# A chunked recurrence in which each chunk starts fourteen steps behind the one before it

## The chip, the cores and the metric

The kernel runs on one core of a Trainium2 chip. The metric is device time of one launch in microseconds. The core has four compute engines, each with its own queue of instructions that it works through in order: TensorE (PE), VectorE (DVE), ScalarE (ACT) and GpSimd (POOL); SyncE (SP) issues most DMAs. Engines wait for one another through semaphores that the program raises and waits for.

## The reference

The model is a block of mixed attention, recurrence, short convolution and an expert lookup, followed by two transformer layers; everything is float32. The change touches only the recurrence of the first block, which runs over 256 context tokens and then 512 latent tokens, in 4 heads of 64 and in both directions:

```python
def step(S, inp):
    r_t, kk_t, v_t, w_t, b_t, k_t = inp
    sa = jnp.einsum('bhij,bhj->bhi', S, kk_t)
    S = S * w_t[:, :, None, :] - sa[..., None] * b_t[:, :, None, :] + v_t[..., None] * k_t[:, :, None, :]
    return S, jnp.einsum('bhij,bhj->bhi', S, r_t)
for d, reverse in enumerate((False, True)):
    ctx_state, y_c = wkv_scan(state0, *c_common, *c_dirs[d], reverse=reverse)
    _, y_l = wkv_scan(ctx_state, *l_common, *l_dirs[d], reverse=reverse)
```

Only the latent tokens' outputs are used; of the context only the state is.

## The kernel before

The recurrence is computed in 12 chunks of 64 tokens, 4 of the context (c = 0 to 3) and 8 latent ones (c = 4 to 11). Both directions and all heads are worked on together, as four 128x128 blocks. A chunk has a part that does not need the state and one that does.

The part without the state (`chunk_pe`, `chunk_act`, `chunk_dve`, `chunk_pool`) goes so:

- Inputs. DVE subtracts the decay sums (L1477), ACT takes exponentials E2, E3, E1 (L1437, L1439, L1441), DVE scales the keys and the queries (L1480, L1484, L1489), POOL scales other keys and copies the values (L1549, L1554), and ACT copies the result into the blocks (L1444).
- PE forms three sets of products, N, M1 and M2 (L1384), four 128x128 matmuls each (for a context chunk M1 and M2 are 64 wide). DVE masks them (L1499, L1502 for N; L1509 and, in latent chunks, L1513 for M1 and M2).
- PE transposes four sets of blocks (L1392: Bt, T0, Kt, Vt) and ACT copies them out of PSUM (L1452).
- The inverse of a triangular matrix follows in four levels l = 1 to 4: products X (L1399), copied by ACT; products A (L1399), added by DVE (L1522); transposes T (L1392), copied by DVE in odd levels (L1526) and by ACT in even ones (L1452). POOL masks the operand of each level (L1541). Last come the products Y and "inverse" (L1399; DVE L1530).

The part with the state (`state_pe`, `state_dve`) has three products with an eviction after each: RH (L1587, L1588; DVE L1627), U (L1595; DVE L1631) and the sum (L1602, L1603; DVE L1635), and then DVE scales the sum into the new state (L1642). A latent chunk also has outputs (L1615 to L1617; DVE L1654). On the profile each float32 matmul counts as two passes, a transpose as one.

Every engine's program for a chunk is a Python generator that yields at the same points, called steps. `chunks` runs two generators by turns, so chunk c and chunk c + 1 are at the same step, and each set of four matmuls of one is followed by the same set of the other. When both have ended, the state parts of c and c + 1 are written one after the other, with the outputs of c between RH and U of c + 1. There are two sets of buffers, and chunk c uses set c % 2, so its inputs wait for the last PE work of chunk c - 2 (`state_filled, (c - 2, "last")`). Each set has its own three PSUM banks; banks 6 and 7 serve the state. A barrier stands before and after the stage.

Of the kernel before, what the change touches and what calls it, by code (L numbers as in the profile page):

```python
# [1369 lines left out]
def chunk_pe(k, p, c):  # L1370
    S, rw = k.S, k.rw
    B, nk = rw.sets[c % 2], 2 if c >= 4 else 1
    yield
    p.wait_ge(S.chunk_kept, (c, "inputs"))
    p.wait_ge(S.chunk_prepared, (c, "inputs"))
    p.wait_ge(S.chunk_copied, (c, "inputs"))
    for step, (name, left, right, w) in enumerate((
            ("N", B.AB, lambda s: B.BB[:, s, :], P),
            ("M1", B.BB, lambda s: B.KR[:, s, 0:nk, :], 64 * nk),
            ("M2", B.KB, lambda s: B.KR[:, s, 0:nk, :], 64 * nk))):  # L1380
        bank = chunk_bank(k, B, c, step)
# [24 lines left out]
    yield
    turned(5, "Kt", B.KB, S.chunk_copied)
    yield
    p.wait_ge(S.chunk_prepared, (c, "values"))
    turned(6, "Vt", B.VB, S.chunk_copied)  # L1410
    yield
    for l in range(1, 5):
        p.wait_ge(S.chunk_prepared, (c, "NTo", l))
        products(4 + 3 * l, f"X{l}", B.NTo, B.Ta, S.chunk_copied)
        yield
        p.wait_ge(S.chunk_copied, (c, f"X{l}"))
        p.wait_ge(S.chunk_copied if l % 2 else S.chunk_kept, (c, f"T{l - 1}"))
        products(5 + 3 * l, f"A{l}", B.Tb, B.Xs, S.chunk_kept)
        yield
        p.wait_ge(S.chunk_kept, (c, f"A{l}"))  # L1420
        turned(6 + 3 * l, f"T{l}", B.Ta, S.chunk_kept if l % 2 else S.chunk_copied)
        yield
    p.wait_ge(S.chunk_copied, (c, "T4"))
    products(19, "Y", B.No, B.Tb, S.chunk_copied)
    yield
    p.wait_ge(S.chunk_copied, (c, "Y"))
    products(20, "inverse", B.Ta, B.Xs, S.chunk_kept)
    yield


def chunk_act(k, p, c):
    S, rw = k.S, k.rw
    B = rw.sets[c % 2]
    if c >= 2:
        p.wait_ge(S.state_filled, (c - 2, "last"))
        p.wait_ge(S.state_ready, c - 2)
    p.e.activation(B.E2, windows(rw.Ls, c), ACT.Exp, scale=-1.0).then_inc(*p.up(S.decay_exp, (c, 2)))  # L1437
    p.wait_ge(S.decay_diff, c)
    p.e.activation(B.E3, B.E3, ACT.Exp).then_inc(*p.up(S.decay_exp, (c, 3)))  # L1439
    if c >= 4:  # L1440
        p.e.activation(B.E1, windows(rw.Ls, c), ACT.Exp).then_inc(*p.up(S.decay_exp, (c, 1)))  # L1441
    p.wait_ge(S.chunk_kept, (c, "keys"))
    for a, h in enumerate(HEAD):
        p.e.activation(B.AB[h, :, h], B.KR[h, :, 0, :], ACT.Copy).then_inc(  # L1444
            *(p.up(S.chunk_copied, (c, "inputs")) if a else p.up(S.scalar_step)))
    if c < 4:
        p.e.activation(B.E1, windows(rw.Ls, c), ACT.Exp).then_inc(*p.up(S.decay_exp, (c, 1)))
    yield

    def copied(step, name, dst):  # L1450
        p.wait_ge(S.chunk_filled, (c, name))
        p.e.activation(flat(dst), chunk_bank(k, B, c, step), ACT.Copy).then_inc(*p.up(S.chunk_copied, (c, name)))  # L1452

    for _ in range(3):
        yield
    for step, name, dst in ((3, "Bt", B.Bt), (4, "T0", B.Tb), (5, "Kt", B.Kt), (6, "Vt", B.Vt)):
        copied(step, name, dst)
        yield
    for l in range(1, 5):
        copied(4 + 3 * l, f"X{l}", B.Xs)  # L1460
        yield
        yield
        if l % 2 == 0:
            copied(6 + 3 * l, f"T{l}", B.Tb)
        yield
    copied(19, "Y", B.Xs)
    yield
    yield


def chunk_dve(k, p, c):
# [14 lines left out]
    if latent:  # L1486
        p.wait_ge(S.decay_exp, (c, 1))
        for d in range(2):
            p.e.tensor_tensor(B.KR[:, SL[d], 1, :], window(rw.Z[:, 0:2, :], c, d), B.E1[:, d], ALU.mult).then_inc(  # L1489
                *(p.up(S.chunk_kept, (c, "inputs")) if d else p.up(S.vector_step)))  # L1490
    else:
        p.in_order()
        p.e.drain().then_inc(*p.up(S.chunk_kept, (c, "inputs")))
    yield
    bank = chunk_bank(k, B, c, 0)
    p.wait_ge(S.chunk_filled, (c, "N"))
# [37 lines left out]
def chunk_pool(k, p, c):  # L1534
# [20 lines left out]
                *(p.up(S.chunk_prepared, (c, "values")) if d and h.start else p.up(S.pool_scaled)))  # L1555
    yield
    yield
    p.wait_ge(S.chunk_kept, (c, "M1", "left") if latent else (c, "M1"))
    off_diagonal(1)
    for _ in range(6):  # L1560
# [13 lines left out]
    return 6 + rw.turn % 2  # L1574


def state_pe(k, p, c, between):

    S, rw = k.S, k.rw
    B, S0 = rw.sets[c % 2], rw.ST[c % 2]  # L1580
    b = state_bank(rw)
    p.claim(("bank", b), S.state_kept, (c, "RH"))
    p.wait_ge(S.state_ready, c - 1)
    p.wait_ge(S.chunk_kept, (c, "inverse"))
    for s in range(4):
        o = k.bank[b][:, s * P:s * P + P]
        p.e.matmul(o, B.M2[:, s, :], B.Vt[:, s, :], start=True, stop=False, skip_group_check=True)  # L1587
        ins = p.e.matmul(o, B.AB[:, s, :], S0[:, s, :], start=False, stop=True, skip_group_check=True)  # L1588
    ins.then_inc(*p.up(S.state_filled, (c, "RH")))
    run(between)  # L1590
    b = state_bank(rw)
    p.wait_ge(S.state_kept, (c, "RH"))
    p.claim(("bank", b), S.state_kept, (c, "U"))
    for s in range(4):
        ins = p.e.matmul(k.bank[b][:, s * P:s * P + P], B.Tb[:, s, :], rw.RH[:, s, :], start=True, stop=True, skip_group_check=True)  # L1595
    ins.then_inc(*p.up(S.state_filled, (c, "U")))
    b = state_bank(rw)
    p.wait_ge(S.state_kept, (c, "U"))
    p.claim(("bank", b), S.state_kept, (c, "sum"))
    for s in range(4):  # L1600
        o = k.bank[b][:, s * P:s * P + P]
        p.e.matmul(o, B.Kt[:, s, :], B.Vt[:, s, :], start=True, stop=False, skip_group_check=True)  # L1602
        ins = p.e.matmul(o, B.Bt[:, s, :], rw.U[:, s, :], start=False, stop=True, skip_group_check=True)  # L1603
    ins.then_inc(*p.up(S.state_filled, (c, "sum" if c >= 4 else "last")))


def outputs_pe(k, p, c):
# [11 lines left out]
    yield  # L1619


def state_dve(k, p, c, between):
    S, rw = k.S, k.rw
    B, S0, S1 = rw.sets[c % 2], rw.ST[c % 2], rw.ST[(c + 1) % 2]
    b = state_bank(rw)
    p.wait_ge(S.state_filled, (c, "RH"))
    p.e.tensor_scalar(flat(rw.RH), k.bank[b], -1.0, None, ALU.mult).then_inc(*p.up(S.state_kept, (c, "RH")))  # L1627
    run(between)
    b = state_bank(rw)
    p.wait_ge(S.state_filled, (c, "U"))  # L1630
    p.e.tensor_copy(flat(rw.U), k.bank[b]).then_inc(*p.up(S.state_kept, (c, "U")))  # L1631
    b = state_bank(rw)
    p.in_order()
    p.wait_ge(S.state_filled, (c, "sum" if c >= 4 else "last"))
# [2 lines left out]
    for s in range(4):  # L1637
        d, g = s // 2, s % 2
        e1 = B.E1[:, d, g, 63:64] if d == 0 else B.E1[:, d, g, 0:1]
        if s == 0:  # L1640
            p.in_order()
        p.e.tensor_scalar(S1[:, s, :], rw.sum[:, s, :], e1, None, ALU.mult).then_inc(  # L1642
            *(p.up(S.state_ready, c) if s == 3 else p.up(S.vector_step)))


def outputs_dve(k, p, c):
# [9 lines left out]
    yield  # L1656


def chunks(k, p, part, state, outputs):

    k.rw.turn = 0
    for c in range(0, 12, 2):
        both = [part(k, p, c), part(k, p, c + 1)]
        while both:
            both = [x for x in both if next(x, x) is not x]
        if state is None:
            continue
# [1926 lines left out]
```

## Time and profile before

| | us |
|---|---|
| median of 3 runs | 4511.9 |
| lowest, highest | 4507.26, 4541.98 |
| profiled execution | 4547.44 |
| its span | 4545.6 |
| mean granted clock of it | 0.855 |

The span is the time from the first to the last instruction in the profiled execution. The twelve chunks lie between 657 us (the first N) and 1028 us of it, after the projections and before the output projection and the expert lookup. A granted clock of 1.00 is 2.4 GHz on TensorE and 0.50 is 1.2 GHz; a value between is a mean over a stretch.

### The profile page before, as it was taken

Reading aid. Unit: us, or ns where it says so; the run is one execution under the profiler, and the core shown is the slowest. Engines: PE = TensorE matmul, PEld = TensorE weight load, DVE = VectorE, ACT = ScalarE, POOL = GpSimd, SP = SyncE. Lnnn points to the kernel's source line nnn. Section 1 sums busy time; section 2 is a strip of 40 time slices with the busy share of each in tenths; the row PEclk is TensorE's granted clock in tenths of the full one; section 3 lists DMA queues with packets and bytes.
Section 4 is the critical chain, followed back from the end, with each engine's and each line's share of the span. In section 5 each row is a group of like instructions: output and inputs, shape, how many; then the busy total and the mean of one; then the engine's idle time right before and its main releaser. Section 6 shows DMA issues by size and latency. Waiting matters only on the chain. (4 is left out here: it accounts for less than half of the span.)

```text
span 4545.6 us, 38958 instructions
## 1 busy us (share of the span) xinstructions
PE 3563.3 (78%) x14192; PEld 2537.7 (56%) x14192; DVE 2238.7 (49%) x4378; ACT 696.2 (15%) x1541; POOL 1408.6 (31%) x1202
## 2 busy tenths in 40 slices
PE   7879957887366667566667898877977889989899
PEld 3446537783122233232545676666765468877687
DVE  2442054443777756755766767777652420032201
ACT  2111022221111111111121101211011210011100
POOL 0640012220266545547534655555520000000000
PEclk9886968998688878888867899978998889997999
DMA  6310300001488878879846899878962024421243
GB/s 193 105 56 5 97 12 1 1 1 48 155 311 311 301 259 298 305 275 370 301 155 240 328 392 360 312 259 299 393 250 65 28 74 148 150 82 38 93 156 104
DMA packets 439283, 833.18 MB, mean 183 GB/s; under 512 B 46451, under 2 KB 281518, under 8 KB 439086
## 3 DMA queue, kind: packets, MB, share of 16 engines
q0 software_dynamic: 147456, 536.94, 32.4%
q1 hardware_dynamic: 291638, 293.76, 20.3%
q8 instruction: 114, 1.87, 0.2%
q14 instruction: 75, 0.61, 0.0%
HBM read 828.44 MB, written 2.17 MB: 183 GB/s over the span
## 5 line engine op out<-in xcount | busy, mean ns | idle before, releaser
L2364 PE MATMUL banks<-arena 128*128 128x256 f32 (+1 forms) x4992 | 1161.0, 392 | 93.6 <-DVE arena L2434 43.4
L2364 PEld LDWEIGHTS banks<-arena 128*128 128x128 f32 (+1 forms) x4992 | 976.8, 197 | 271.9 <-issue 67.3
L1953 POOL DMA_INDIRECT arena<-in_peer_v,arena x512 | 637.4, 1245 | 785.9 <-DVE arena L2062 468.2
L2073 DVE CUSTOM_DVE_ANT_0 arena<-arena 128x1024 f32<-128x1024 f32 x512 | 628.1, 1227 | 236.5 <-DMA arena<-in_peer_u,arena 221.0
L2020 PE MATMUL banks<-arena 128*128 128x512 f32 x768 | 449.7, 729 | 298.0 <-ACT arena L2038 181.7
L1953 POOL DMA_INDIRECT arena<-in_peer_u,arena x512 | 554.9, 1084 | 378.4 <-DVE arena L1905 187.7
L2020 PEld LDWEIGHTS banks<-arena 128*128 128x128 f32 x768 | 166.3, 230 | 552.8 <-issue 330.9
L2062 DVE SCALAR_TENSOR_TENSOR arena<-arena 128x1024 f32<-128x1024 f32 x316 | 406.2, 1285 | 34.9 <-DMA arena<-in_peer_v,arena 25.0
L614 PE MATMUL banks<-arena 128*128 128x512 f32 (+1 forms) x768 | 312.7, 566 | 1.8 <-DVEq L280 1.8
L3130 PE MATMUL banks<-arena 128*128 128x256 f32 x1408 | 310.4, 378 | 0.0
L3172 DVE TENSOR_TENSOR arena<-banks,arena 128x512 f32<-128x512 f32 x44 | 30.5, 692 | 528.1 <-PE banks L2364 527.7
L3130 PEld LDWEIGHTS banks<-arena 128*128 128x128 f32 x1408 | 265.6, 189 | 38.3
L614 PEld LDWEIGHTS banks<-arena 128*128 128x128 f32 x768 | 149.7, 196 | 163.3 <-issue 158.1
L958 PE MATMUL banks<-arena 128*128 128x512 f32 (+1 forms) x320 | 131.1, 557 | 25.4 <-ACT arena L1085 9.8
L2626 PE MATMUL banks<-arena 64*128 64x256 f32 (+6 forms) x384 | 142.6, 482 | 4.4 <-issue 3.2
L2633 PE MATMUL banks<-arena 128*128 128x128 f32 x360 | 87.6, 344 | 65.4 <-ACT arena L2684 34.4
L2640 PE MATMUL banks<-arena 128*128 128x64 f32 (+1 forms) x720 | 134.8, 330 | 2.2 <-DVE arena L2735 2.2
L2640 PEld LDWEIGHTS banks<-arena 128*128 128x128 f32 x720 | 131.0, 259 | 6.0 <-issue 4.8
L3151 ACT ACTIVATE arena<-banks 128x512 f32<-128x512 f32 x44 | 26.3, 597 | 700.0 <-PE banks L2364 699.9
L2669 ACT ACTIVATE arena<-arena 128x256 f32<-128x256 f32 (+3 forms) x128 | 69.4, 542 | 393.3 <-DVE arena L2708 299.2
L2633 PEld LDWEIGHTS banks<-arena 128*128 128x128 f32 x360 | 52.1, 171 | 120.5 <-issue 62.4
L513 POOL TENSOR_TENSOR arena<-arena 128x2048 f32<-128x2048 f32 x16 | 57.3, 3602 | 196.5 <-ACTq L280 104.9
(327 smaller groups left out, 3900.5 us busy)
## 6 DMA issues: line engine op xcount, KB each, us to landing
arena<-in_l_w_gate SPq DMA_DIRECT2D x44, 1024.0 KB, 7.4
arena<-in_l_w_up SPq DMA_DIRECT2D x44, 1024.0 KB, 9.0
arena<-in_l_w_down SPq DMA_DIRECT2D x44, 1024.0 KB, 6.5
arena<-in_ada_w SPq DMA_DIRECT2D x24, 1024.0 KB, 8.5
arena<-in_l_w_qkv SPq DMA_DIRECT2D x24, 1024.0 KB, 6.3
arena<-in_w_in SPq DMA_DIRECT2D x36, 512.0 KB, 4.0
arena<-in_l_w_out SPq DMA_DIRECT2D x16, 1024.0 KB, 5.2
arena<-in_peer_q_w SPq DMA_DIRECT2D x16, 512.0 KB, 4.8
```

The costliest lines, as they stand in the source:

```text
L614: ins = p.e.matmul(k.bank[b][0:m, 0:n], k.W[slot][:, c, 0:m], rhs(c), start=c == 0, stop=c == c_n - 1, skip_group_check=True)
L958: ins = p.e.matmul(k.bank[b][0:m, 0:n], k.W[slot][:, c, 0:m], rhs(c), start=c == 0, stop=c == c_n - 1, skip_group_check=True)
L1953: p.e.indirect_dma_start(e.ring[slot], None, tables[table], bass.IndirectOffsetOnAxis(ap=e.IDX[h][:, t, j:j + 1], axis=0)).then_inc(*p.up( ...
L2020: ins = p.e.matmul(k.bank[b], e.diag[x % 4], e.ring[slot][:, half * T:half * T + T], start=h == 0 and j == 0, stop=h == HEADS - 1 and j == ...
L2062: p.e.scalar_tensor_tensor(out=e.ACC[t], in0=e.ring[slot], scalar=factor, in1=e.ACC[t], op0=ALU.mult, op1=ALU.add).then_inc(*p.up(S.rows_a ...
L2073: p.e.tensor_tensor_reduce(out=e.prod, in0=e.ring[slot], in1=e.H2[:, t, :], scale=1.0, scalar=0.0, op0=ALU.mult, op1=ALU.add, accum_out=e. ...
L2364: ins = p.e.matmul(out, left(c), right(c), start=c == 0, stop=c == c_n - 1, skip_group_check=True)
L2626: ins = p.e.matmul(k.bank[b][:, c0:c0 + keys.shape[1]], x.q, keys, start=True, stop=True, skip_group_check=True)
L2633: ins = p.e.transpose(k.bank[4][:, j * P:j * P + P], a.S[u % 2][:, j * P:j * P + P], k.ident)
L2640: ins = p.e.matmul(k.bank[5][:, 0:x.w], a.PT[u % 2][:, j * P:j * P + P], values, start=j == 0, stop=j == len(x.values) - 1, skip_group_che ...
L2669: p.e.activation(s[:, 0:x.nb], s[:, 0:x.nb], ACT.Exp, bias=low, scale=-1.0, accum_out=cols[:, 2:3]).then_inc(*(p.up(S.weights_exp, key) if ...
L3130: ins = p.e.matmul(k.bank[4 + o // 2][:, o % 2 * TH:o % 2 * TH + TH], w[:, r, P * o:P * o + P], a.hid[:, (i - 1) % 2, TH * r:TH * r + TH], ...
```

## The change

A chunk's generator now goes on through its state part and its outputs: `state_pe` and `state_dve` yield after each of their products, where the outputs of another chunk used to be passed in. `chunks` keeps a list of active chunks. Chunk c joins it at step 14c, and at each step the older one is written before the newer. One step is added near the start of each engine's program of a chunk: PE forms N in a chunk's third step now, two steps after DVE's first work on the inputs, and on ACT the copies into the blocks are a step of their own.

```diff
--- before.py
+++ after.py
@@ -1371,6 +1371,7 @@
     S, rw = k.S, k.rw
     B, nk = rw.sets[c % 2], 2 if c >= 4 else 1
     yield
+    yield
     p.wait_ge(S.chunk_kept, (c, "inputs"))
     p.wait_ge(S.chunk_prepared, (c, "inputs"))
     p.wait_ge(S.chunk_copied, (c, "inputs"))
@@ -1439,6 +1440,7 @@
     p.e.activation(B.E3, B.E3, ACT.Exp).then_inc(*p.up(S.decay_exp, (c, 3)))
     if c >= 4:
         p.e.activation(B.E1, windows(rw.Ls, c), ACT.Exp).then_inc(*p.up(S.decay_exp, (c, 1)))
+    yield
     p.wait_ge(S.chunk_kept, (c, "keys"))
     for a, h in enumerate(HEAD):
         p.e.activation(B.AB[h, :, h], B.KR[h, :, 0, :], ACT.Copy).then_inc(
...
@@ -1587,13 +1591,14 @@
         p.e.matmul(o, B.M2[:, s, :], B.Vt[:, s, :], start=True, stop=False, skip_group_check=True)
         ins = p.e.matmul(o, B.AB[:, s, :], S0[:, s, :], start=False, stop=True, skip_group_check=True)
     ins.then_inc(*p.up(S.state_filled, (c, "RH")))
-    run(between)
+    yield
     b = state_bank(rw)
     p.wait_ge(S.state_kept, (c, "RH"))
     p.claim(("bank", b), S.state_kept, (c, "U"))
     for s in range(4):
         ins = p.e.matmul(k.bank[b][:, s * P:s * P + P], B.Tb[:, s, :], rw.RH[:, s, :], start=True, stop=True, skip_group_check=True)
     ins.then_inc(*p.up(S.state_filled, (c, "U")))
+    yield
     b = state_bank(rw)
...
+LAG = 14
+
+
+def pauses_of(n):
+    for _ in range(n):
+        yield
+
+
+def chunk_steps(k, p, c, part, state, outputs):
+
+    yield from part(k, p, c)
+    if state is None:
+        yield from pauses_of(4 if c >= 4 else 3)
+        return
+    yield from state(k, p, c)
+    if c >= 4:
+        yield from outputs(k, p, c)
+
+
 def chunks(k, p, part, state, outputs):
 
     k.rw.turn = 0
-    for c in range(0, 12, 2):
-        both = [part(k, p, c), part(k, p, c + 1)]
-        while both:
-            both = [x for x in both if next(x, x) is not x]
-        if state is None:
-            continue
-        state(k, p, c, None)
-        state(k, p, c + 1, outputs(k, p, c) if c >= 4 else None)
-        if c >= 4:
-            run(outputs(k, p, c + 1))
+    active, step, c = [], 0, 0
+    while active or c < 12:
+        if c < 12 and step >= c * LAG:
+            active.append(chunk_steps(k, p, c, part, state, outputs))
+            c += 1
+        active = [x for x in active if next(x, x) is not x]
+        assert len(active) < 3
+        step += 1
```

The first place is PE's queue where a latent pair begins. A row is a line, an operation and how many of it follow one another; L1384 (now L1385) is N, M1 and M2, L1392 (now L1393) transposes, L1399 (now L1400) the products of the levels. Before:

```order
L1384 MATMUL banks<-arena 128x128 x24
L1392 MATMUL banks<-arena 128x128 x32
L1399 MATMUL banks<-arena 128x128 x16
L1392 MATMUL banks<-arena 128x128 x8
L1399 MATMUL banks<-arena 128x128 x16
L1392 MATMUL banks<-arena 128x128 x8
```

and with the change, from X2 and A2 of the older chunk on:

```order
L1400 MATMUL banks<-arena 128x128 x8
L1393 MATMUL banks<-arena 128x128 x4
L1400 MATMUL banks<-arena 128x128 x8
L1385 MATMUL banks<-arena 128x128 x4
L1393 MATMUL banks<-arena 128x128 x4
L1385 MATMUL banks<-arena 128x128 x4
L1400 MATMUL banks<-arena 128x128 x4
L1385 MATMUL banks<-arena 128x128 x4
L1400 MATMUL banks<-arena 128x128 x4
L1393 MATMUL banks<-arena 128x128 x12
L1400 MATMUL banks<-arena 128x128 x4
L1393 MATMUL banks<-arena 128x128 x4
```

N, M1 and M2 stood together for both chunks, then all first transposes, then level after level. Now T2, X3 and A3 of the older chunk stand ahead of N of the newer, and M1 and M2 are divided by T3 and X4.

The second place is DVE's queue at the same point. L1477 to L1489 (now L1479 to L1491) prepare inputs, L1499 and L1502 (L1502 and L1505) evict N, L1509 and L1513 (L1512 and L1516) evict M1 and M2, L1522 (L1525) adds A, L1529 copies T of an odd level. Before:

```order
L1477 TENSOR_TENSOR arena<-arena 128x256
L1480 TENSOR_TENSOR arena<-arena 64x4x64 x2
L1484 TENSOR_TENSOR arena<-arena 128x2x64 x2
L1489 TENSOR_TENSOR arena<-arena 128x2x64 x2
L1477 TENSOR_TENSOR arena<-arena 128x256
L1480 TENSOR_TENSOR arena<-arena 64x4x64 x2
L1484 TENSOR_TENSOR arena<-arena 128x2x64 x2
L1489 TENSOR_TENSOR arena<-arena 128x2x64 x2
L1499 TENSOR_TENSOR arena<-banks,arena 128x512 x2
L1502 TENSOR_TENSOR arena<-arena 128x512
L1499 TENSOR_TENSOR arena<-banks,arena 128x512 x2
L1502 TENSOR_TENSOR arena<-arena 128x512
```

and with the change, from the addition of the older chunk's A2 on:

```order
L1525 TENSOR_TENSOR arena<-banks,arena 128x512
L1479 TENSOR_TENSOR arena<-arena 128x256
L1482 TENSOR_TENSOR arena<-arena 64x4x64 x2
L1486 TENSOR_TENSOR arena<-arena 128x2x64 x2
L1491 TENSOR_TENSOR arena<-arena 128x2x64 x2
L1525 TENSOR_TENSOR arena<-banks,arena 128x512
L1502 TENSOR_TENSOR arena<-banks,arena 128x512 x2
L1505 TENSOR_TENSOR arena<-arena 128x512
L1529 COPY arena<-banks 128x512
L1512 TENSOR_TENSOR arena<-banks,arena 64x4x64 x2
L1516 TENSOR_TENSOR arena<-banks,arena 128x256
L1512 TENSOR_TENSOR arena<-banks,arena 64x4x64 x2
```

The additions of A2 and A3 of the older chunk stand around the inputs of the newer, and its copy of T3 stands between the evictions of N and M1.

## Rows read from the trace of the kernel before

**Rows 1.** The page, part 1: busy us, share of the span, number of instructions.
```profile
PE 3563.3 (78%) x14192; PEld 2537.7 (56%) x14192; DVE 2238.7 (49%) x4378; ACT 696.2 (15%) x1541; POOL 1408.6 (31%) x1202
```

**Rows 2.** Windows by round: stretch, its length, busy time of each engine, granted clock, DMA.
```profile
657.00:719.00 62.00, 50.05 (x352) 47.23 (x352) 26.88 (x52) 16.45 (x32) 14.67 (x21) 0.86 0.00 1
719.00:783.00 64.00, 52.48 (x352) 49.44 (x352) 26.40 (x52) 16.41 (x32) 14.33 (x20) 0.82 0.00 1
783.00:847.20 64.20, 53.08 (x400) 50.41 (x401) 31.25 (x68) 17.06 (x35) 14.47 (x20) 0.88 0.00 1
847.20:908.60 61.40, 51.14 (x401) 48.34 (x401) 30.28 (x64) 16.43 (x33) 14.48 (x20) 0.92 0.00 1
...
970.00:1027.80 57.80, 51.05 (x400) 48.23 (x400) 27.20 (x54) 14.21 (x27) 11.88 (x14) 0.93 0.00 1
```

**Rows 3.** Timeline of PE, fourth round: start, length, line, passes, idle time before.
```profile
847.22 2.05 PE L1384 MATMUL banks<-arena 128*128 128x128 f32 x8 [3.45 <-ACT arena L1444]
850.80 6.73 PE L1384 MATMUL banks<-arena 128*128 128x128 f32 x40 [1.53 <-ACT arena L1444]
857.37 2.35 PE L1392 MATMUL banks<-arena 128*128 128x128 f32 x20
...
861.27 3.80 PE L1399 MATMUL banks<-arena 128*128 128x128 f32 x32
864.96 0.66 PE L1392 MATMUL banks<-arena 128*128 128x128 f32 x4
865.85 0.66 PE L1392 MATMUL banks<-arena 128*128 128x128 f32 x4 [0.24 <-DVE arena L1522]
866.35 3.80 PE L1399 MATMUL banks<-arena 128*128 128x128 f32 x32
...
888.20 1.16 PE L1595 MATMUL banks<-arena 128*128 128x128 f32 x8 [0.78 <-DVE arena L1627]
```

**Rows 4.** Timeline of DVE, same stretch.
```profile
847.54 1.29 DVE L1480 TENSOR_TENSOR arena<-arena 64x256 f32<-64x256 f32 x2 [0.50 <-ACT arena L1437]
848.86 0.91 DVE L1484 TENSOR_TENSOR arena<-arena 128x128 f32<-128x128 f32 x2
849.69 0.57 DVE L1489 TENSOR_TENSOR arena<-arena 128x128 f32<-128x128 f32 x2
850.19 1.27 DVE L1499 TENSOR_TENSOR arena<-banks,arena 128x512 f32<-128x512 f32 x2
851.50 0.69 DVE L1502 TENSOR_TENSOR arena<-arena 128x512 f32<-128x512 f32 x1
...
856.05 0.86 DVE L1509 TENSOR_TENSOR arena<-banks,arena 64x256 f32<-64x256 f32 x2
856.95 0.42 DVE L1513 TENSOR_TENSOR arena<-banks,arena 128x256 f32<-128x256 f32 x1
...
865.11 0.69 DVE L1522 TENSOR_TENSOR arena<-banks,arena 128x512 f32<-128x512 f32 x1 [0.20 <-PE banks L1399]
```

**Rows 5.** Timeline of ACT, same stretch.
```profile
847.10 0.42 ACT L1437 ACTIVATE arena<-arena 128x256 f32<-128x256 f32 x1
...
849.80 0.85 ACT L1444 ACTIVATE arena<-arena 64x256 f32<-64x256 f32 x2 [1.68 <-DVE arena L1484]
...
863.26 0.60 ACT L1452 ACTIVATE arena<-banks 128x512 f32<-128x512 f32 x1 [0.30 <-PE banks L1399]
```

**Rows 6.** Windows around a round start and two state phases: the granted clock.
```profile
847.00:857.00 10.00, 8.25 (x45) 8.01 (x46) 8.55 (x19) 1.93 (x6) 4.24 (x8) 0.60 0.00 0
857.00:865.00 8.00, 7.80 (x70) 7.49 (x69) 3.42 (x8) 5.33 (x10) 3.27 (x3) 1.00 0.01 2
...
885.00:894.00 9.00, 5.67 (x45) 4.95 (x43) 3.89 (x9) 0.00 (x0) 0.00 (x0) 1.00 0.00 0
...
764.00:770.00 6.00, 4.70 (x24) 4.22 (x24) 1.04 (x3) 0.00 (x0) 0.00 (x0) 0.72 0.00 0
```

**Rows 7.** POOL's level masks in the stage, from the groups by line.
```profile
L1541 POOL TENSOR_TENSOR arena<-arena 128x512 f32<-128x512 f32 x48 | 52.4, 1091 | 98.3 <-PE banks L1399 66.0 <-DVE arena L1509 29.2
```

More of the change, by code:

```diff
@@ L1574, in state_bank, with state_pe @@
     return 6 + rw.turn % 2
-def state_pe(k, p, c, between):
+def state_pe(k, p, c):
     S, rw = k.S, k.rw
@@ L1596, in state_pe @@
     ins.then_inc(*p.up(S.state_filled, (c, "U")))
+    yield
     b = state_bank(rw)
@@ L1604, in state_pe @@
     ins.then_inc(*p.up(S.state_filled, (c, "sum" if c >= 4 else "last")))
+    yield
 def outputs_pe(k, p, c):
@@ L1619, in outputs_pe, with state_dve @@
     yield
-def state_dve(k, p, c, between):
+def state_dve(k, p, c):
     S, rw = k.S, k.rw
@@ L1627, in state_dve @@
     p.e.tensor_scalar(flat(rw.RH), k.bank[b], -1.0, None, ALU.mult).then_inc(*p.up(S.state_kept, (c, "RH")))
-    run(between)
+    yield
     b = state_bank(rw)
@@ L1631, in state_dve @@
     p.e.tensor_copy(flat(rw.U), k.bank[b]).then_inc(*p.up(S.state_kept, (c, "U")))
+    yield
     b = state_bank(rw)
@@ L1643, in state_dve @@
             *(p.up(S.state_ready, c) if s == 3 else p.up(S.vector_step)))
+    yield
 def outputs_dve(k, p, c):
@@ L1656, in outputs_dve @@
     yield
+LAG = 14
+def pauses_of(n):
+    for _ in range(n):
+        yield
+def chunk_steps(k, p, c, part, state, outputs):
[6 more added lines that the diff above has]
+        yield from outputs(k, p, c)
 def chunks(k, p, part, state, outputs):
     k.rw.turn = 0
-    for c in range(0, 12, 2):
-        both = [part(k, p, c), part(k, p, c + 1)]
-        while both:
-            both = [x for x in both if next(x, x) is not x]
-        if state is None:
-            continue
-        state(k, p, c, None)
-        state(k, p, c + 1, outputs(k, p, c) if c >= 4 else None)
-        if c >= 4:
-            run(outputs(k, p, c + 1))
+    active, step, c = [], 0, 0
[6 more added lines that the diff above has]
+        step += 1
 def rwkv_output_pe(k, p):
```

## The prediction

> **What bounds the kernel now.** The page's first part says how much there is to win: TensorE is busy for 78% of the span, more than any other engine [rows 1]. A window for each of the six rounds of the recurrence then gives its size, 62.0 + 64.0 + 64.2 + 61.4 + 61.4 + 57.8 = 370.8 us, 8% of the span [rows 2] (the fifth round repeats the fourth). A full round holds 51.1 us of PE work in 61.4 us [rows 2]; DVE has 30, POOL 14, ACT 16. So no other engine bounds it, and what could go is the 10.3 us of PE idleness and the part of the 51.1 that runs at half clock. The timeline of PE shows where both lie. A round begins with 3.45 us without work, then N of chunk A, 8 passes in 2.05 us, 1.53 us without work, and 40 passes in 6.73 us [rows 3]; later 32 passes go in 3.69 us (861.27 to 864.96). The granted clock agrees: 0.60 from 847 to 857, 1.00 from 857 to 865 [rows 6]. Half speed thus costs 8.8 us less 48 x 0.112 = 5.4, or 3.4 us per latent round. The rest of the idleness is 0.24 us per level and the state's hand-offs, as the 0.78 us before U [rows 3]. At full clock the work of a latent chunk is (51.1 - 3.4)/2 = 23.9 us.
>
> **The change, part by part.** No instruction of arithmetic is added or removed; no DMA is issued in the stage. Only the order on the four engines changes. Two things are gained: the state's steps and the outputs of one chunk stand between steps of the next, and the inputs of a chunk are prepared while another has work. Three are lost: X and A of a chunk no longer have the partner's same step between them and their eviction at every place, each chunk prepares its inputs by itself (eleven handovers and not five), and the first and the last chunk run alone for 14 steps each.
>
> Durations for the walk:
> - eight passes 0.9 us (a quarter of the 32 passes in 3.69, [rows 3]); a group of four transposes 0.5 (865.85 to 866.35); state products twice 0.9, outputs 2.65 (24 passes at 0.11)
> - A to its transposes: the products end at 864.85 (four groups from 861.27), the addition begins at 865.11 and takes 0.69, the transposes start at 865.85: 1.0 [rows 3, 4]. X or a transpose to ACT and back: 0.2 + 0.6 + 0.06 [rows 5]
> - inputs: from the first exponential at 847.10 to PE's start at 850.80, 3.7 us, with 1.29, 0.91 and 0.57 on DVE between [rows 3 to 5]
> - DVE for N: 850.19 to 852.2, 2.0; each mask pair with its row part 1.25 [rows 4]; POOL 1.1 for a level's mask [rows 7]
>
> Steady state, two latent chunks, time 0 at the end of A2 of the older one c. In that step c-1 has just ended, and c+1 has nothing on PE for its first two steps. So T2 waits for its addition with no cover: 1.0 to 1.5; X3 to 2.4. ACT copies T2 at 1.7 and only then computes the exponentials of c+1, from 2.3; the copy of X3 stands behind them and ends at 4.0. A3 runs 4.06 to 4.95. N of c+1 comes at 2.33 + 3.7 = 6.03. Idle so far: 1.0 + 1.7 + 1.1. N, T3, M1, X4 and M2 then follow without a hole to 10.2, A4 and Bt to 11.7. DVE is behind: queued after the keys' products (5.5) it does A3's addition (6.2), N's three (from 7.2 to 9.2), the copy of T3 (9.9), and the masks of M1 (11.15) and M2 (12.4), and only then A4's addition (13.1). T4 starts at 13.15: idle 1.45. T0 follows, Y waits 0.4 for T4's copy (14.5 to 15.4), Kt, inverse 16.26 to 17.15, Vt, RH 18.15 (0.4 idle) to 20.0, X1 to 20.9, U to 21.9, A1 to 22.8, sum to 24.8, T1, outputs 25.4 to 28.1, X2 to 29.0, and A2 after X2's copy, 29.85 to 30.75. **The period is 30.75 us per chunk, where a round gave 61.4/2 = 30.7** [rows 2]. The state is hidden as meant (RH's eviction lies under X1, U's under A1, the sum's under T1 and the outputs), but waits of about 7 us per chunk stand where 10.3/2 = 5.2 us stood; the half clock's 1.7 us per chunk pays for the difference.
>
> With no outputs the period is 2.65 shorter, and with a context chunk as the newer one DVE's masks are 4 x 0.4 us shorter, of which 1.4 lie on the way to A4's addition. So three periods of 26.7 (chunks 0 to 2 older), one of 28.1 (3 older, 4 newer), seven of 30.75: 80.1 + 28.1 + 215.3 = 323.5 us.
>
> The ends. Chunk 0 alone, at half clock, since PE had stood still before: N 2.05, masks to about +6.3 and the transposes to +8.3, then X1 1.75, 0.86, A1 1.75, 1.0, T1 0.8, X2 1.75, 0.86, A2 1.75: 18.8 us. Chunk 11 alone after its A2: two levels at 0.9 + 0.86 + 0.9 + 1.0 + 0.5 less what overlaps to T4's end (9.8), copy 0.86, Y 0.9, copy 0.86, inverse 0.9, addition 1.0, RH 1.85, 1.0, U 0.9, 1.05, sum 1.85, outputs 2.65: 23.6 us. Sum 18.8 + 323.5 + 23.6 = 365.9 us.
>
> The clock. It fell in every round after PE had waited 3.45 us, and it also fell in a state phase, with no wait there longer than U's 0.78 us [rows 3]: 0.72 on average over the 6 us from 764 to 770, so 3.4 us at half [rows 6]. In the handover above PE waits 3.8 us in three pieces over 6 us, with no piece above 1.7; from 885 to 894, busy 5.67 of 9 us, the fourth round kept the clock [rows 6]. The two speak against one another, so I take the fall at half of the eleven handovers, for the 3.4 us of the shorter case, 1.7 us lost each: 9 us. Bounds: 0 and, if each is as long as at a round's start (847.22 to 857.37, 10.2 us, [rows 3]), 11 x 5.1 = 56. For the lone ends I add 2 (0 to 6). Together 376.9, against 370.8: **+6 us**. What else the walk may miss I bound at -1.5 and +1.5 us per period, since every duration in it comes from a row, and only the gaps between engines are read to 0.1 us: -16 and +16.
>
> The profiled execution lasted 4547.4 us (span 4545.6), 35.5 above the median 4511.9. The stage is as long whatever the rest does, so I add 6 to the median: 4518. Before's own runs lie 35 us apart; within 1%, or 45 us, nothing can be told from no change.
>
> **Rivals.**
> 1. *Forecast, 0.68.* Same within 1%: 4518, own range 4495 to 4542.
> 2. *The clock falls at every handover and stays low, 0.12.* For it: all six rounds begin as the fourth does, and the handovers are now eleven. Against: the stretch from 885 that kept 1.00 [rows 6]. Each costs 10.2/2 = 5.1, in all 56 in place of my 9: +53, 4565 us. It decides once the falls cost more than 4.5 us each: 11 x 4.5 - 9 + 6 = 46. Twenty transposes ran in 2.35 us, at full rate, with twelve more behind them before 861.27, and the stretch stayed at 1.00 [rows 3, 6]: 3.9 us of transposes alone did not drop the clock. The Trainium skill, "TensorE: Matmul & The Clock Gate", Part 4, holds that transposes do not count as work for the clock; by that rule this rival's time is the likely one, since T2 and Bt, T4, T0 lie among the waits. The trace doesn't bear it out.
> 3. *Waits shorter than walked and no fall, 0.08.* If ACT's and DVE's queues at the handover cost only what the state's hand-offs cost (0.8 twice in place of 3.8 and 1.45), a period is 27.1: 365.9 - 11 x 3.65 = 325.7, or -45: 4467. For: PE's work is only 23.9. Against: ACT's exponentials stand ahead of X3's copy in its queue.
> 4. *A milder form of 3, 0.10.* The clock holds and a period is 1 us shorter: 355, -16: 4496.
> 5. *The lag does not free the buffers in time, 0.02.* If c+2 waited for c's outputs it would be near lockstep again. But c ends at step 26 and c+2 begins at step 28, so only a slip of an engine could do it: 4512.
>
> **Range and chances.** 4485 to 4555 holds cases 1, 4 and 5 and the milder half of 2. Faster by over 1%: case 3, 0.08. Slower: case 2, 0.12. Same: 0.80.
>
> **What would show it.** Right: gaps of PE ahead of T2, A3 and N at each handover of 1.0, 1.7 and 1.1 us; T4 waiting on DVE by about 1.4; state hand-offs without idleness; starts of N 30 to 32 us apart in the latent part; a stage of 360 to 385 us. Wrong: a stage under 350 or over 400, N starts under 28 apart, or a granted clock below 0.8 across the latent part. What breaks it first is the clock at the handovers.

## The result

The change made no gain: the median went from 4521.1 us (20 runs) to 4543.0 (20 runs), and the ratio is 1.004 with a 95% interval of 1.0021 to 1.0058. By that ratio the changed kernel is about 18 us slower (9 to 26), by the medians 22. That is more than the noise of so many runs and less than the 1% that the prediction calls no change. The forecast was 4518 against the 4511.9 that was the median of the kernel before at that time, or +6; 4543.0 lies inside the range of 4485 to 4555, in its upper part.

The stage can be measured by itself in the two profiled executions. These are the windows ahead of it, of it and behind it; the columns are the stretch, its length, busy time of PE, weight loads, DVE, ACT and POOL, granted clock, and DMA. Of the changed kernel:

```profile
0.00:637.40 637.40, 515.02 (x1746) 291.79 (x1747) 218.69 (x410) 113.31 (x253) 131.97 (x64) 0.86 0.29 84
637.40:1019.60 382.20, 311.56 (x2304) 288.68 (x2304) 180.60 (x353) 96.32 (x188) 86.69 (x115) 0.92 0.00 1
1019.60:4532.40 3512.80, 2717.75 (x10142) 1943.90 (x10142) 1851.41 (x3615) 486.12 (x1101) 1190.53 (x1024) 0.85 0.63 222
```

and of the kernel before:

```profile
0.00:657.00 657.00, 534.44 (x1746) 304.73 (x1746) 214.78 (x411) 113.27 (x253) 131.97 (x63) 0.83 0.28 81
657.00:1027.80 370.80, 308.76 (x2304) 291.89 (x2304) 172.29 (x352) 96.76 (x188) 84.30 (x115) 0.88 0.00 1
1027.80:4545.60 3517.80, 2720.11 (x10143) 1941.13 (x10142) 1851.58 (x3615) 486.14 (x1101) 1192.32 (x1024) 0.86 0.63 222
```

The stage went from 370.8 to 382.2 us, +11.4, with the same 2304 passes and at a higher clock, 0.92 for 0.88. The rest went from 4174.8 to 4150.2, though nothing in it changed. Over the eleven profiles of this study it lies between 4137 and 4179 us. So one profiled time says little about this stage, and the stage's own length says more. Its +11.4 us lies within the interval of the whole kernel (9 to 26 us).

A period is the time from one chunk's N to the next chunk's, and a handover is the place around N where the newer chunk joins the older. The starts of N of the twelve chunks lie 21.9, 29.5, 30.3, 30.3, 31.3, 31.7, 32.0, 30.8, 30.8, 31.8 and 31.7 us apart, and 50.1 us follow. Counted against 30.8 us for each of twelve chunks (369.6), the last chunk has 19.3 us more, the first period 8.9 less, the four periods after it 1.8 less in sum, and the six latent ones 4.0 more: so the excess lies at the ends, where a chunk runs alone, and in the falls of the clock. A full period at full clock on PE, where a row is start, length, line, passes and the idleness before them:

```profile
875.31 1.13 PE L1385 MATMUL banks<-arena 128*128 128x128 f32 x8 [0.99 <-ACT arena L1446]
...
882.42 1.09 PE L1393 MATMUL banks<-arena 128*128 128x128 f32 x8 [1.47 <-DVE arena L1525]
883.76 1.16 PE L1400 MATMUL banks<-arena 128*128 128x128 f32 x8 [0.25 <-ACT arena L1454]
...
899.14 1.16 PE L1400 MATMUL banks<-arena 128*128 128x128 f32 x8 [0.69 <-ACT arena L1454]
901.08 0.66 PE L1393 MATMUL banks<-arena 128*128 128x128 f32 x4 [0.78 <-DVE arena L1525]
...
903.95 1.16 PE L1400 MATMUL banks<-arena 128*128 128x128 f32 x8 [1.33 <-ACT arena L1454]
906.09 1.12 PE L1385 MATMUL banks<-arena 128*128 128x128 f32 x6 [0.98 <-ACT arena L1446]
```

Of [rows 3], the 3.45 us ahead of N and the round's slow passes are gone: N goes in 1.13 us for 8 passes after 0.99 us. In their place stand 0.78 ahead of T2, 1.33 ahead of A3, 0.98 ahead of N, 1.47 ahead of T4, and 0.69 ahead of A2. The period is 30.78 us (875.31 to 906.09), half a round was 30.7. At the handovers to chunks 2 to 5, where the state just formed is a context chunk's, so that no outputs stand between its sum and A2, something else happens:

```profile
772.99 1.57 PE L1400 MATMUL banks<-arena 128*128 128x128 f32 x8 [2.00 <-DVE arena L1529]
775.34 1.12 PE L1393 MATMUL banks<-arena 128*128 128x128 f32 x4 [0.78 <-DVE arena L1525]
776.24 1.92 PE L1400 MATMUL banks<-arena 128*128 128x128 f32 x8
778.85 2.07 PE L1400 MATMUL banks<-arena 128*128 128x128 f32 x8 [0.69 <-ACT arena L1454]
780.81 2.05 PE L1385 MATMUL banks<-arena 128*128 128x128 f32 x8
```

A2 waits 2.00 us for DVE, and in it passes begin to take twice as long (N 2.05). The slow passes partly fill what were waits: A3 waits 0.69 here for 1.33 above, and N not at all for 0.98. The granted clock of four stretches of the changed kernel, two at such handovers, one at a later T4 and one without a fall:

```profile
681.00:692.00 11.00, 9.53 (x45) 8.90 (x45) 5.07 (x9) 3.05 (x7) 4.10 (x7) 0.53 0.00 0
742.00:753.00 11.00, 9.53 (x45) 8.92 (x46) 5.91 (x12) 2.94 (x7) 4.24 (x7) 0.54 0.01 1
820.00:826.00 6.00, 5.38 (x31) 4.67 (x29) 0.69 (x1) 2.61 (x5) 0.00 (x0) 0.72 0.00 0
869.00:880.00 11.00, 7.90 (x66) 7.36 (x65) 7.89 (x16) 3.53 (x8) 4.29 (x8) 1.00 0.00 1
```

Of the eleven handovers, four (681 to 784) had about 10 us at half clock each and two later ones 3.4 us; two more falls of 3.4 us came at a T4, and five handovers had none. The same waits of a latent handover, 0.69, 0.78, 1.33 and 0.98 us, stood ahead of a fall at 906 and kept 1.00 at 875, so the waits alone don't tell which.

### The profile page after: what moved, and what is told of

It reads as the page before. It is cut to its first block and busy times, and to the rows that moved or that the text cites. A ratio compares the mean times of both kernels' runs of the same rounds, so it can differ in the third digit from the quotient of the medians.

```text
span 4532.4 us, 38940 instructions
## 1 busy us (share of the span) xinstructions
PE 3544.3 (78%) x14192; PEld 2524.4 (56%) x14192; DVE 2250.7 (50%) x4378; ACT 695.7 (15%) x1541; POOL 1409.2 (31%) x1202
## 5 line engine op out<-in xcount | busy, mean ns | idle before, releaser
L2045 PEld LDWEIGHTS banks<-arena 128*128 128x128 f32 x768 | 164.5, 228 | 550.1 <-issue 323.5
L3155 PEld LDWEIGHTS banks<-arena 128*128 128x128 f32 x1408 | 265.6, 189 | 38.3
L614 PEld LDWEIGHTS banks<-arena 128*128 128x128 f32 x768 | 147.9, 193 | 160.6 <-issue 155.4
L1400 PE MATMUL banks<-arena 128*128 128x128 f32 x960 | 144.9, 298 | 33.5 <-ACT arena L1454 25.5
L1400 PEld LDWEIGHTS banks<-arena 128*128 128x128 f32 x960 | 127.4, 207 | 44.4 <-ACT arena L1454 35.8
L2658 PE MATMUL banks<-arena 128*128 128x128 f32 x360 | 87.8, 344 | 65.5 <-ACT arena L2709 34.5
L2665 PEld LDWEIGHTS banks<-arena 128*128 128x128 f32 x720 | 131.3, 259 | 6.2 <-issue 5.0
```

Source lines behind the costliest of these rows:

```text
L614: ins = p.e.matmul(k.bank[b][0:m, 0:n], k.W[slot][:, c, 0:m], rhs(c), start=c == 0, stop=c == c_n - 1, skip_group_check=True)
L2045: ins = p.e.matmul(k.bank[b], e.diag[x % 4], e.ring[slot][:, half * T:half * T + T], start=h == 0 and j == 0, stop=h == HEADS - 1 and j == ...
L2658: ins = p.e.transpose(k.bank[4][:, j * P:j * P + P], a.S[u % 2][:, j * P:j * P + P], k.ident)
L2665: ins = p.e.matmul(k.bank[5][:, 0:x.w], a.PT[u % 2][:, j * P:j * P + P], values, start=j == 0, stop=j == len(x.values) - 1, skip_group_che ...
L3155: ins = p.e.matmul(k.bank[4 + o // 2][:, o % 2 * TH:o % 2 * TH + TH], w[:, r, P * o:P * o + P], a.hid[:, (i - 1) % 2, TH * r:TH * r + TH], ...
```

## The experiments

Every kernel was timed or profiled beside the kernel before on its chip. "Stage" is the first N to the end of the last outputs in the profile.

| kernel | ratio to before, 95% interval | stage, us | granted clock | latent period, us |
|---|---|---|---|---|
| before | | 370.8 | 0.88 | 30.7 (half a round) |
| changed | 1.004, 1.0021 to 1.0058 | 382.2 | 0.92 | 30.8 |
| one more step behind the inputs (e_early) | 0.9991, 0.9965 to 1.0018 | 358.7 | 0.96 | 29.2 |
| T1 and T3 copied by ACT (e_tact) | 0.9969, 0.9943 to 0.9995 | 364.2 | 0.97 | 30.2 |
| filler in the waits (e_busy) | 1.0033, 1.0009 to 1.0057 | 377.8 | 0.96 | 30.8 |
| both (e_both) | 0.9927, 0.9905 to 0.9949 | 342.2 | 0.99 | 28.6 |
| both and filler (e_bothbusy) | 0.9921, 0.9895 to 0.9947 | 342.2 | 0.99 | 28.6 |
| before, with filler (e_beforefill) | 0.9987, 0.9964 to 1.001 | 358.7 | 0.97 | 30.6 (half a round) |
| lag of 28 (e_lag28) | one run, 4664.0 us | 500.3 | 0.91 | 41.9 |
| lag of 16 (e_lag16) | one run, 4572.7 us | 392.1 | 0.99 | 32.7 |
| POOL's mask held back (e_port) | one run, 4540.8 us | 369.2 | 0.97 | 30.8 |

The theories: (1) the chain of waits at the handover and in DVE's queue sets the period; (2) the clock does; (3) the loss lies outside the stage. The third is out: the stage itself is 11.4 us longer, and in each kernel of the table that has an interval the stage's difference from 370.8 lies inside the interval of the whole.

**The inputs a step earlier.** One `yield` more in each of the four programs of a chunk, behind its first work, as on ACT:

```diff
         p.e.activation(B.E1, windows(rw.Ls, c), ACT.Exp).then_inc(*p.up(S.decay_exp, (c, 1)))
     yield
+    yield
     p.wait_ge(S.chunk_kept, (c, "keys"))
```

> The changed kernel with one more step behind each chunk's work on its inputs, on all four engines, so that the exponentials of a chunk stand in ACT's queue ahead of T2's copy of the older chunk and not behind it. The stage from the first N to the last outputs took 382.2 us with the change and 370.8 before. If the chain of waits at the handover (theory 1) makes the loss: A3 comes 0.8 us and N 1.6 us earlier, so 11 x 1.6 = 18 us less, a stage of 364 and a time about 18 us under the change's. If the half clock makes it (theory 2): less idleness at the handover also ends most falls, so another 10 to 20 us less, stage 345 to 355. If the loss lies outside the stage (theory 3): the stage gets shorter but the time stays at 4540.

PE's timeline at a handover (A2, T2, A3) and at T4:

```profile
798.18 1.16 PE L1401 MATMUL banks<-arena 128*128 128x128 f32 x8 [0.69 <-ACT arena L1456]
800.12 0.66 PE L1394 MATMUL banks<-arena 128*128 128x128 f32 x4 [0.79 <-DVE arena L1528]
...
802.42 1.16 PE L1401 MATMUL banks<-arena 128*128 128x128 f32 x8 [0.76 <-ACT arena L1456]
...
810.66 1.09 PE L1394 MATMUL banks<-arena 128*128 128x128 f32 x8 [1.48 <-DVE arena L1528]
```

The wait ahead of A3 is 0.76 in place of 1.33, and N has none; 0.78 ahead of T2 and 1.48 ahead of T4 stand as they did. 0.57 + 0.98 = 1.55, and the period fell by 1.6 to 29.2. Theory 1 holds to 0.1 us for the latent period. The stage came to 358.7, between theory 1's 364 and theory 2's 345 to 355. About 27 us of it ran at half clock in place of 64, so there is something in theory 2 too. The median is 4532.7 against 4531.5 for before; the interval of the ratio (-16 to +8 us) holds the stage's -12 us as well as no gain, and can't confirm it.

**T1 and T3 copied by ACT.** DVE's queue loses the copy that stood behind its scalings of the state and behind the evictions of N.

```diff
-        p.wait_ge(S.chunk_copied if l % 2 else S.chunk_kept, (c, f"T{l - 1}"))
+        p.wait_ge(S.chunk_copied, (c, f"T{l - 1}"))
...
-        if l % 2 == 0:
-            copied(6 + 3 * l, f"T{l}", B.Tb)
+        copied(6 + 3 * l, f"T{l}", B.Tb)
```

> The changed kernel with the copies of T1 and T3 on ACT in place of DVE, no change of steps. Theory 1, waits in the chain: A2 of the newer chunk no longer waits 2.0 us for T1's copy behind DVE's sum and scalings but about 0.9 for X2's copy, and T4 waits some 0.6 less for A4's addition, which stood behind T3's copy: 11 x 1.7 = 19 us less, stage 363. Theory 2, the clock: these waits are not at the place where it falls except that A2 stands just ahead of it, so the stage is shorter by what the waits give and the falls stay: 370 or more. ACT gets 24 copies of 0.6 us more, beside PE's work.

PE's timeline, A3 and T4:

```profile
925.85 1.16 PE L1400 MATMUL banks<-arena 128*128 128x128 f32 x8 [1.33 <-ACT arena L1454]
...
934.51 1.09 PE L1393 MATMUL banks<-arena 128*128 128x128 f32 x8 [0.88 <-DVE arena L1524]
```

T4 waits 0.88 in place of 1.47, and the latent period fell by just that, to 30.2. The expected 1.7 us per period was wrong for the latent chunks: there A2's wait had been 0.69 all along, as the sum's 2.65 us of outputs hide DVE. The 2.0 us were a matter of the handovers to chunks 2 to 5, where the periods went from 29.5 to 31.3 down to 28.4, 26.8, 26.9 and 29.0. Theory 2's expectation that the falls would stay is refuted: about 21 us of half clock are left. T4's shorter wait makes 3.5 us over six latent periods, of the 18 that the stage gained; the rest lies in the context periods and in falls that did not come.

**Filler in the waits.**

```diff
+        if l == 2:
+            p.claim(chunk_place(B, c, 12), S.chunk_copied, (c, "T2"))
+            fill(k, p, B.ring[((c // 2) * STEPS + 12) % 3], 4)
         p.wait_ge(S.chunk_kept, (c, f"A{l}"))
```

and in the same way 6 ahead of A3 and 4 ahead of N; `fill` issues matmuls of the identity.

> The changed kernel with matmuls of the identity with itself put into the waits ahead of T2 (4), A3 (6) and N (4) of every chunk, into banks that the next real product overwrites; nothing reads them. PE is busy through the handover, the chain of waits is as it was. Theory 1: the granted clock is 1.00 across the stage and what goes is the half rate alone, seven falls of which four lasted 10 us, so 4 x 4 + 3 x 1.7 = 21 us at most, less what the filler adds where a wait was shorter than it (11 x 0.5): stage 366 to 375. Theory 2: the period falls to 28 and the stage to under 355. If filler at half clock delays the real work instead, the stage is over 382.

PE's timeline; L1373 is the filler, L1396 N, and L1405 T4 and T0:

```profile
869.39 1.50 PE L1373 MATMUL banks<-arena 128*128 128x128 f32 x12
...
871.88 1.06 PE L1373 MATMUL banks<-arena 128*128 128x128 f32 x8
873.04 1.13 PE L1396 MATMUL banks<-arena 128*128 128x128 f32 x8
...
880.15 1.09 PE L1405 MATMUL banks<-arena 128*128 128x128 f32 x8 [1.47 <-DVE arena L1544]
```

PE had next to no idleness at the handover, the clock stayed at 1.00 over the last five periods, and each was 30.8 us, as the changed kernel's periods without a fall. A full clock leaves the period where it was, which rules theory 2 out as what sets the latent period. The falls themselves did not all go: the stage's clock was 0.96 and not 1.00, A2 still waited 2.00 us without filler ahead of it at the handover at 771 us, and one period of 32.0 us had filler at half clock in it. The stage gained 4.4 us and stayed above the expected 366 to 375.

**No overlap.** `LAG = 28`.

> The changed kernel with a lag of 28 steps in place of 14, so that no two chunks overlap and each runs as chunk 11's end did. It measures what a chunk costs alone. The last chunk took 50.0 us from N to the end of its outputs, with 13 us of that beside another. Theory 1: the chain from inputs to outputs alone is 43 to 48 us for a latent chunk at full clock and about 38 for a context chunk, 8 x 46 + 4 x 38 = 520, stage 500 to 560 and a time 120 to 180 us over the change's. Theory 2: PE is busy for under half of it, the clock falls for good, and the stage is over 600.

A level and the next chunk's N on PE:

```profile
906.36 1.16 PE L1400 MATMUL banks<-arena 128*128 128x128 f32 x8 [0.69 <-ACT arena L1454]
908.30 0.66 PE L1393 MATMUL banks<-arena 128*128 128x128 f32 x4 [0.78 <-DVE arena L1525]
...
938.95 5.45 PE L1385 MATMUL banks<-arena 128*128 128x128 f32 x24 [3.46 <-ACT arena L1446]
```

A chunk alone takes 41.9 us, at a granted clock of 0.91 over the stage: a latent one less than the 43 to 48 expected and a context one more than 38, with 0.69 and 0.78 us of waits a level and 3.46 ahead of N. The stage of 500.3 is at the lower edge of theory 1's 500 to 560, far from theory 2's 600. Overlap by the lag saves 41.9 - 30.8 = 11.1 us a chunk; lockstep in pairs saves 11.2. Those two numbers sum up the case: the change exchanges one way to cover waits for another that covers as much, and adds 14 steps without a partner at each end.

**Both changes, with and without filler.**

> The step added behind the inputs and the copies of T1 and T3 on ACT, together. In the profiles the undisturbed latent period was 30.8 us with the change, 29.2 with the step alone and 30.2 with the copies alone. Theory 1 (the chain of waits sets the period, and these are two places in it): the gains add, 30.8 - 1.6 - 0.6 = 28.6 us, so a stage of about 352 and a time 10 to 20 us under before's. Theory 2 (the clock decides): what both gained came from fewer falls, 27 and 21 us of half clock in place of 64, and there is little left, so stage 357 to 360 as with the step alone.

> The same with fillers of three matmuls of the identity ahead of T2 and of A3, whose result nothing reads, and none ahead of N. Theory 1: the period stays at 28.6 us, only falls of the clock go, 0 to 10 us of the stage: 342 to 352. Theory 2: over 10 us less than without the filler.

PE's timeline of the first, T2, A3, N (L1386) and T4:

```profile
868.11 0.66 PE L1394 MATMUL banks<-arena 128*128 128x128 f32 x4 [0.79 <-DVE arena L1527]
...
870.41 1.16 PE L1401 MATMUL banks<-arena 128*128 128x128 f32 x8 [0.75 <-ACT arena L1456]
871.51 1.16 PE L1386 MATMUL banks<-arena 128*128 128x128 f32 x8
...
878.05 1.09 PE L1394 MATMUL banks<-arena 128*128 128x128 f32 x8 [0.88 <-DVE arena L1527]
```

The two gains add to a latent period of 28.6 us as forecast. The stage came to 342 and not to the 352 forecast, since the context periods fell too, to 25.4 us (25.9 for the last), and only the first 10 us of the stage ran at half clock. That is also why the filler changes nothing. The stage is 28.6 us shorter than before's, and the ratio of 0.9927 is a gain of 0.7%, small but clear of noise. The changed kernel is slower than before, so this version beats both.

**The kernel before with filler** ahead of each pair's N, from the second pair on.

```diff
+    if c >= 2:
+        p.claim(chunk_place(B, c, 0), S.chunk_kept, (c, "filler"))
+        fill(k, p, B.ring[((c // 2) * STEPS) % 3], 6 if c % 2 else 14)
     p.wait_ge(S.chunk_kept, (c, "inputs"))
```

> The kernel before the change with fillers of the same kind ahead of the N of each pair from the second on, 14 matmuls for the first chunk and 6 for the second, whose result nothing reads. A round lost 3.4 us of a latent round, and more of a context round, to half clock after PE's waits of 3.45 and 1.53 us. If the clock falls because PE waits there, the latent rounds go from 61.4 to 58 us and the stage from 370.8 to about 348, and this beats the change by 30 us. If it falls for another reason, the rounds stay at 61.4, or get longer by filler that runs at half clock: stage 371 to 385.

PE's timeline at a round's start (L1373 is filler) and the window of it:

```profile
833.85 3.34 PE L1373 MATMUL banks<-arena 128*128 128x128 f32 x28
837.47 1.13 PE L1396 MATMUL banks<-arena 128*128 128x128 f32 x8 [0.28 <-ACT arena L1456]
838.43 1.50 PE L1373 MATMUL banks<-arena 128*128 128x128 f32 x12
841.06 4.70 PE L1396 MATMUL banks<-arena 128*128 128x128 f32 x40 [1.12 <-ACT arena L1456]
...
848.14 0.66 PE L1404 MATMUL banks<-arena 128*128 128x128 f32 x4 [0.58 <-DVE arena L1525]
...
850.74 3.80 PE L1411 MATMUL banks<-arena 128*128 128x128 f32 x32
```

```profile
837.00:847.00 10.00, 8.60 (x75) 8.21 (x74) 9.25 (x20) 2.95 (x8) 4.77 (x8) 1.00 0.01 2
```

N goes in 1.13 us for 2.05 and the 40 passes in 4.70 for 6.73 [rows 3], at 1.00 for 0.60 [rows 6]: the clock had fallen because PE waited there. But the first products X come 13.27 us after N (850.74 less 837.47) where they came after 14.05 [rows 3]: of the 3.4 us at half clock only 0.8 lay on the path. DVE, busy for 9.25 of these 10 us, makes the transposes wait twice 0.58. This round and the next were 61.7 and 60.7 us long where 61.4 stood before and 58 was expected. The stage's 12 us come from the second round, 56.3 us for 64.0, and the third, 60.5 for 64.2. What the prediction counted as the price of a latent round's half clock was the passes' extra time, not the round's.

**A lag of 16.** `LAG = 16`.

> The changed kernel with a lag of 16 steps. Other steps meet, and two more of a chunk's 27 have no partner. Theory 1: each period is longer by what two steps take without cover, 2 to 3.5 us, so 33 to 34 us and a stage of 405 to 420, unless the handover falls better, when at least the added steps' own work of 1.8 us remains. Theory 2: more idleness brings more falls, periods of 35 and a stage over 420.

PE's timeline of N, the transposes and A's transposes:

```profile
870.92 1.13 PE L1385 MATMUL banks<-arena 128*128 128x128 f32 x8 [1.52 <-DVE arena L1529]
...
874.96 0.66 PE L1393 MATMUL banks<-arena 128*128 128x128 f32 x4 [1.12 <-DVE arena L1525]
...
892.23 0.66 PE L1393 MATMUL banks<-arena 128*128 128x128 f32 x4 [0.78 <-DVE arena L1525]
```

The period is 32.7 us, +1.9: much as the 1.8 us of work in two steps, though the waits stand elsewhere (1.52 us ahead of N, 1.12 ahead of T). At a clock of 0.99 the stage came to 392 and not to 405. PE did nothing for 98 of these 392 us, against 71 of 382 in the changed kernel, and yet the clock fell less. How long PE waits in all does not decide on the falls; theory 2 expected the opposite. This is one run.

**POOL's mask held back.** At the handovers to chunks 2 to 5 DVE's four scalings took longer, 1.75 us for 0.88. From the timeline of all engines of the changed kernel at one of them:

```profile
770.49 1.75 DVE L1649 TENSOR_SCALAR arena<-arena 128x128 f32<-128x128 f32 x4
...
771.07 1.09 POOL L1544 TENSOR_TENSOR arena<-arena 128x512 f32<-128x512 f32 x1 [4.13 <-PE banks L1400]
772.16 0.68 DVE L1529 COPY arena<-banks 128x512 f32<-128x512 f32 x1
```

```diff
+            if l == 2 and c:
+                p.wait_ge(S.state_ready, c - 1)
             p.wait_ge(S.chunk_filled, (c, f"X{l}"))
             off_diagonal(l + 1)
```

> The changed kernel, but POOL's level mask after X2 waits until DVE has scaled the older chunk's state (it has 3 us to spare there). In the changed kernel one of the four scalings took 1.16 us in place of 0.28 at the first four handovers and ended as POOL's mask did (771.07 + 1.09 us). Theory 1a: the two share something that one must wait for; then the four scalings take 0.88 us again, T1's copy ends 0.87 us earlier, and A2's wait of 2.0 us at the first four handovers is 1.1. The stage is then 3.5 us shorter, or up to 15 if the clock no longer falls there. Theory 1b: DVE was held by something else, as PSUM or ACT; the scalings stay at 1.75 us and the wait at 2.0.

DVE's scalings, POOL's mask and PE's A2 of this kernel:

```profile
773.39 0.88 DVE L1651 TENSOR_SCALAR arena<-arena 128x128 f32<-128x128 f32 x4
```

```profile
774.35 1.09 POOL L1544 TENSOR_TENSOR arena<-arena 128x512 f32<-128x512 f32 x1 [4.50 <-DVE arena L1651]
```

```profile
775.02 1.13 PE L1400 MATMUL banks<-arena 128*128 128x128 f32 x8 [1.12 <-DVE arena L1529]
```

The scalings take 0.88 us again and A2 waits 1.12, at all four places. Theory 1a is confirmed: DVE was held while POOL's mask ran. The stage was 13 us shorter in this one run. Of these, 4 x 0.87 = 3.5 are the wait; most of the rest is half clock that did not come, and not all of that can be put down to the mask. 4.1 us of it lie in the latent periods, where nothing was held in either kernel, and without the hold the clock still fell at two of the four handovers (0.50 from 692 to 698 us, 0.66 from 752 to 757).

This kernel also has a context period at a clock of 1.00, from N of chunk 3 to N of chunk 4. T4, A2, A3 and N of it on PE:

```profile
724.84 1.13 PE L1385 MATMUL banks<-arena 128*128 128x128 f32 x8 [1.29 <-DVE arena L1525]
...
731.16 1.09 PE L1393 MATMUL banks<-arena 128*128 128x128 f32 x8 [0.69 <-DVE arena L1525]
...
745.64 1.13 PE L1400 MATMUL banks<-arena 128*128 128x128 f32 x8 [1.12 <-DVE arena L1529]
...
750.29 1.16 PE L1400 MATMUL banks<-arena 128*128 128x128 f32 x8 [1.19 <-ACT arena L1454]
752.43 1.69 PE L1385 MATMUL banks<-arena 128*128 128x128 f32 x8 [0.99 <-ACT arena L1446]
```

It is 27.6 us long.

## Why the prediction was right

The forecast of no change within 1% was right, and so was the reason for it: the new order covers as much of a latent chunk's waits as the old one. The stage was forecast at +6 us and came to +11.4. By the prediction's own steps:

- *The period.* 30.75 us was walked and 30.78 measured. Its waits, walked and measured: T2 1.0 and 0.78; A3 1.7 and 1.33; N 1.1 and 0.98; T4 1.45 and 1.47; Y and inverse 0.4 and 0.3, 0.25 each; RH 0.4 and 0.44; A2 0.85 and 0.69. The measured ones sum to 6.2 us and the walked ones to 7.2. Most of that 1 us is a matter of counting and no error: the walk lets eight passes end after 0.9 us, the profile about 0.2 us later (861.27 + 3.80 = 865.07 where the walk takes 864.85, [rows 3]), so that PE's busy time is as much longer as its waits are shorter. That these waits make the period was shown by removing some of them (e_early, e_tact, and their sum in e_both), and that the clock doesn't was shown by e_busy.
- *The context periods were mis-sized.* "With no outputs the period is 2.65 shorter" is the step that was furthest off. 26.7 us was forecast three times and 28.1 once; measured were 29.5, 30.3, 30.3 and 31.3, or 13.2 us more in sum. The periods of 26.7 came out longer for three reasons. The order itself gives 27.6, the period at full clock in e_port: PE's work is 2.7 us less than in a latent period, but A2 waits 1.12 for 0.69, since without outputs ahead of it DVE's sum, scalings and copy of T1 are no longer hidden, and T4's wait falls from 1.47 only to 0.69, where the lighter masks were to save all of it but 0.05. POOL's mask held the scalings for another 0.87 us. Half clock added the remaining 1.1 to 1.9 us. The hold stands nowhere in the prediction, and half clock was a term of its own. e_port removed the hold, and e_tact and e_both the copy; in e_both three of the context periods are 25.4.
- *The clock.* The 9 us for falls came out about right in sum, and that is luck. Half of eleven handovers were to have falls of 3.4 us that cost 1.7 each. There were eight falls, four of them of 10 us, and each cost less than the extra time of its passes, since the slow passes fill waits: the latent periods with a fall were 31.7 to 32.0 us, 0.9 to 1.2 above those without, and half clock cost 1.1 to 1.9 us in each of the three context periods that can be compared, and not the 5.1 a handover of the second rival. By an estimate from these numbers that is about 4 us in the latent periods and 6 in the context ones. Half clock in the stage was about 64 us, in before about 85. "The half clock's 1.7 us per chunk pays for the difference" explains why an equal period could have more waits in it, and is not borne out: e_beforefill puts it at 0.8 us from N to X1 of a latent round, 0.4 a chunk. The second rival, a fall at every handover, was so in four of the first five handovers and in two of the six after them.
- *The ends.* The first N to the second took 21.9 us, where the walk has 24.8, as the clock came back earlier than assumed (a mean of 0.78 over the stretch, so some 10 us at half clock). The tail took 50.1, where it has 48.3; in e_port, without a fall in it, it was 48.9.
- *Sum.* Without the clock the walk had 365.9. Deviations, with the falls in them: -2.9 first, +13.2 context, +4.3 latent, +1.8 tail: 382.3. With its clock term of 11 the forecast missed by 5 us.
- *The rule weighed.* For its second rival the prediction weighs the rule of the Trainium skill, "TensorE: Matmul & The Clock Gate", Part 4, that transposes do not count as work for the clock. The traces lean against it and don't settle it: in the kernel before PE ran a block of 32 transposes from 731.78 to 737.14 us, and the granted clock rose over it, 0.50 from 719 to 732, 0.70 from 732 to 738 and 1.00 from 738 to 750. The time that the prediction read from the rule, 4565 us with 5.1 lost at every handover, did not come either. Why two later falls came at a T4, among transposes, and why most T4's had none, stays open.

## What to carry to other kernels

Two ways to cover the same waits compete: here each saved about 11 us a chunk. So before a software pipeline replaces lockstep, walk one period on all queues, and look for what stands behind the new work in the in-order queues of the evicting engines. The gain here came when the exponentials were moved ahead of one copy and another copy to a less busy engine (stage 382 to 342 us). Walk the odd part of the loop too: a shorter body, here the context chunks without outputs, uncovers what the full body hides. And where a profile of the whole program varies by 40 us outside the stage, compare the stage's own length.

## What the runs showed of the hardware

- A DVE `tensor_scalar` from SBUF to SBUF, 0.28 us by itself, took 1.16 us when it started at 771.1 us, just after a POOL `tensor_tensor` had started at 771.07, and it ended within 0.1 us of it (771.07 + 1.09 = 772.16). When POOL's instruction was held back until the scalings were done, all 48 of them took 0.28 to 0.29 us (e_port). The Trainium skill, "GPSIMD Engine Reference", in its table of the engine, has the SBUF interfaces shared with VectorE, with contention for DVE instructions in a two-port mode or with two SBUF inputs. The Trainium skill, "VectorE: DVE Perf Modes", "Mode 2×_2P", puts single-source SBUF instructions such as `tensor_scalar` in such a mode. The hold in the trace agrees with the two; which mode the instruction ran in, no trace shows.
- The clock fell with no single wait above 2.0 us: at a handover after 2.00 us, with 0.78 and 0.69 us to follow between groups of 4 and 8 passes. Waits of 0.69, 0.78, 1.33 and 0.98 us kept 1.00 from 868 to 876 and stood ahead of a fall at 906. Filler whose result nobody reads kept it up (e_beforefill 1.00 for 0.60). It shortened the second and third rounds by 7.7 and 3.7 us and left the other four within 0.7 us of what they were.
